# Two-layer decoder trunk on one core: weights laid out by the host unit by unit, one transfer for each unit of 1 MB

## The reference

```python
f = swiglu(rms_norm(h, ffn1_pre_g[i]), ffn1_w_gu[i], ffn1_w_down[i])
h = h + 0.5 * rms_norm(f, ffn1_post_g[i])
u = rms_norm(h, mix_pre_g[i])
sb_q, sb_k, sb_v, df_q, df_k, df_v, g_sb, g_df = jnp.split(u @ w_in[i], split_at, axis=-1)
...
merged = jax.nn.sigmoid(g_sb) * y_sb + jax.nn.sigmoid(g_df) * y_df
h = h + rms_norm(merged @ w_out[i], mix_post_g[i])
f = swiglu(rms_norm(h, ffn2_pre_g[i]), ffn2_w_gu[i], ffn2_w_down[i])
h = h + 0.5 * rms_norm(f, ffn2_post_g[i])
gate = jax.nn.sigmoid(rms_norm(h, ple_pre_g[i]) @ w_ple_gate[i])
h = h + rms_norm((p[i] @ w_ple_proj[i]) * gate, ple_post_g[i])
```

## Time and profile before

| what | before |
|---|---|
| median of 3 runs | 1174.02 us (1173.8 to 1174.78) |
| span of the profiled execution, first to last instruction | 1172.6 us |
| median of the runs less that span | 1.4 us |
| TensorE busy | 1164.0 us (99%) |
| VectorE, ScalarE, GpSimd busy | 850.0, 721.0, 53.0 us |
| DMA | 215.37 MB, mean 184 GB/s, 138655 packets |
| of these, packets under 2 KB | 97904 |

### The profile page before, as it was taken

The page is one execution under the profiler, slowest core; times in us unless marked ns, Lnnn a source line. Parts: engine busy times, 40 slices in busy tenths (PEclk is TensorE's granted clock), DMA queues, the critical chain, the costliest instruction groups (busy, mean ns, idle before and its releaser), DMA issues.

```text
span 1172.6 us, 17196 instructions
## 1 busy us (share of the span) xinstructions
PE 1164.0 (99%) x6031; PEld 983.8 (84%) x6031; DVE 850.0 (72%) x1290; ACT 721.0 (61%) x1166; POOL 53.0 (5%) x124
## 2 busy tenths in 40 slices
PE   9999999999999999999999999999999999999997
PEld 7888888888888888888888888888888888888886
DVE  6766776977857776676787776678776677677666
ACT  7555556577755755555685655565776566565555
POOL 4000000000000000000100000010000010000002
PEclk9999999999999999999999999999999999999999
DMA  9656564654354555655556565746434446546550
GB/s 296 217 181 212 171 215 164 226 172 152 121 201 146 191 204 185 208 174 211 179 171 198 172 211 179 240 165 198 171 111 179 162 162 215 194 170 209 179 196 37
DMA packets 138655, 215.37 MB, mean 184 GB/s; under 512 B 6958, under 2 KB 97904, under 8 KB 138608
## 3 DMA queue, kind: packets, MB, share of 16 engines
q1 hardware_dynamic: 135808, 208.43, 52.6%
q10 hardware_dynamic: 2576, 6.29, 1.6%
q0 software_dynamic: 224, 0.04, 0.0%
HBM read 213.68 MB, written 1.05 MB: 183 GB/s over the span
## 4 chain that ended last, share of the span: by engine, by line
PE 99%; DMA 0%; DVE 0%; ACT 0%; issue 0%; POOL 0%; POOLq 0%; DVEq 0%; ACTq 0%
PE ps L1673 23%; PE ps L1546 19%; PE ps L1548 18%; PE ps L1547 18%; PE ps L1683 12%; PE ps L1916 3%; PE ps L1593 1%; PE ps L1925 1%; PE ps L1802 1%; PE ps L1817 1%; PE ps L1776 0%; PE ps L1788 0%; DMA raw<-in_w_ple_proj 0%; PE ps L1831 0%; PE ps L1838 0%; PE ps L1803 0%
## 5 line engine op out<-in xcount | busy, mean ns | idle before, releaser
L1106 DVE SCALAR_TENSOR_TENSOR w_lo<-raw,g_layer,w_hi 128x512 fp32r<-128x512 f32 (+1 forms) x504 | 356.3, 767 | 139.2 <-ACT w_hi L644 139.2
L644 ACT ACTIVATE w_hi<-raw,g_layer 128x512 fp32r<-128x512 f32 (+1 forms) x524 | 346.7, 732 | 113.6 <-PE ps L1683 97.0
L1673 PE MATMUL ps<-x_both,w_hi 128*128 128x512 f32 x1152 | 287.7, 392 | 0.0
L1673 PEld LDWEIGHTS ps<-x_both,w_hi 128*128 128x128 f32 x1152 | 209.3, 189 | 39.4 <-issue 0.4
L1546 PE MATMUL ps<-w_hi,x_both 128*128 128x512 f32 x576 | 231.6, 402 | 0.0
L1548 PE MATMUL ps<-w_hi,x_both 128*128 128x512 f32 x576 | 225.0, 391 | 0.0
L1547 PE MATMUL ps<-w_lo,x_both 128*128 128x512 f32 x576 | 224.4, 390 | 0.0
L1103 DVE TENSOR_TENSOR w_lo<-raw,w_hi 128x1024 fp32r<-128x1024 f32 x114 | 134.8, 1221 | 61.3 <-ACT w_hi L641 61.3
L641 ACT ACTIVATE w_hi<-raw 128x1024 fp32r<-128x1024 f32 x114 | 114.7, 1053 | 92.7 <-PE ps L1548 92.5
L1683 PEld LDWEIGHTS ps<-x_both,w_lo 128*128 128x128 f32 x1152 | 152.6, 191 | 8.4
L1683 PE MATMUL ps<-x_both,w_lo 128*128 128x256 f32 x1152 | 156.0, 283 | 0.0
(11 more groups left out here) (230 smaller groups left out, 1041.7 us busy)
## 6 DMA issues: line engine op xcount, KB each, us to landing
raw<-in_ffn_w_gu SPq DMA_DIRECT2D x170, 512.0 KB, 4.6
raw<-in_ffn_w_down SPq DMA_DIRECT2D x88, 512.0 KB, 4.0
raw<-in_w_in SPq DMA_DIRECT2D x80, 512.0 KB, 4.5
raw<-in_w_out SPq DMA_DIRECT2D x16, 512.0 KB, 4.1
raw<-in_w_ple_gate SPq DMA_DIRECT2D x16, 512.0 KB, 4.1
raw<-in_w_branch_sb SPq DMA_DIRECT2D x8, 512.0 KB, 4.1
raw<-in_w_branch_diff SPq DMA_DIRECT2D x8, 512.0 KB, 4.2
raw<-in_ffn_w_gu SPq DMA_DIRECT2D x12, 256.0 KB, 7.8
```

The lines of the kernel that those rows point to most:

```text
L644: last = act.activation(w_hi[:, s, part], raw[:, s, part], ACT.Copy, scale=g_layer[:, g:g + 1])
L1106: last = dve.scalar_tensor_tensor(out=w_lo[:, s, part], in0=raw[:, s, part], scalar=g_layer[:, g:g + 1], in1=whi[:, part], op0=ALU.mult, o ...
L1673: mm = pe.matmul(dst, w_hi[:, s, cols], x_both[:, :, 4 * half + k, :], start=half == 0 and k == 0, stop=stop and k == 3, skip_group_check= ...
```

## The change

The ten weight arrays are no longer inputs of the kernel one by one. The host copies them into one array `units` of shape (198, 128, 2048): the 1 MB of a unit lies in one block, and each partition's 2048 values lie in one row of 8 KB, in the order in which the `raw` slot holds them. `load` then issues one DMA of 1 MB for each unit in place of two of 512 KB, and `arrived` counts 16 for each unit in place of 32. The pieces of the first four units stay 256 KB, but each is now 128 rows of 2 KB, for units 1 to 3 too; the rows of a piece lie 8 KB apart in HBM. Slots, waits, the order of the loads, and everything on ScalarE, VectorE and TensorE but the count and the source of two DMAs stay as they are.

```diff
         def arrived(i, u, c=0):
-            return 32 * (UNITS // SLOTS) * i + 32 * c + 32 * (u // SLOTS + 1 - len(range(slot(u), PIECED, SLOTS)))
+            return 16 * (UNITS // SLOTS) * i + 16 * c + 16 * (u // SLOTS + 1 - len(range(slot(u), PIECED, SLOTS)))
...
-        def proj_piece(k):
-            return a["w_ple_proj"][0, (k % 2) * P:(k % 2 + 1) * P, (k // 2) * W:(k // 2 + 1) * W]
+        def unit_of(i, u):
+            return a["units"][i * UNITS + u, :, :]
...
-            def load(i, u, parts, c=0):
+            def load(i, u, c=0):
                 sp_.wait_ge(split_done, UNITS * i + 3 * c + u + 1)
-                for dst, src in parts:
-                    sp_.dma_start(dst, src).then_inc(raw_in[slot(u)], 16)
+                sp_.dma_start(raw[:, slot(u), :], a["units"][bass.ds(3 * c + (i * UNITS + u), 1), :, :].rearrange(
+                    "o p n -> p (o n)")).then_inc(raw_in[slot(u)], 16)
...
             def load_pieces(u, ks=range(4)):
                 for k in ks:
-                    dst = raw[:, slot(u), piece(u, k)]
                     if u == PIECED - 1:
                         sp_.wait_ge(split_done, u + 1)
-                    if u == U_PROJ:
-                        src = proj_piece(k)
-                    else:
-                        c, row = divmod(u - U_FFN1, 2)
-                        dst = dst.rearrange("p (g n) -> p g n", g=2)
-                        src = a["ffn1_w_gu"][0, (4 * row + k) * P:(4 * row + k + 1) * P, :].rearrange(
-                            "p (g n) -> p g n", g=2)[:, :, c * FC:(c + 1) * FC]
-                    sp_.dma_start(dst, src).then_inc(piece_in[u][k], 16)
+                    sp_.dma_start(raw[:, slot(u), piece(u, k)], unit_of(0, u)[:, piece(u, k)]).then_inc(piece_in[u][k], 16)
...
         def _(act):
             for k in (0, 2):
-                act.dma_start(raw[:, slot(U_PROJ), piece(U_PROJ, k)], proj_piece(k)).then_inc(piece_in[U_PROJ][k], 16)
+                act.dma_start(raw[:, slot(U_PROJ), piece(U_PROJ, k)], unit_of(0, U_PROJ)[:, piece(U_PROJ, k)]).then_inc(piece_in[U_PROJ][k], 16)
...
+def laid_units(inputs):
...
+    def deep(name, i, row):
+        units.append(w[name][i, row:row + 2 * P, :].reshape(2, P, D).transpose(1, 0, 2))
+
+    def gate_up(name, i, step, half):
+        rows = w[name][i, half * 4 * P:(half + 1) * 4 * P, :].reshape(4, P, 2, FF)
+        units.append(rows[:, :, :, step * FC:(step + 1) * FC].transpose(1, 0, 2, 3))
...
+    return np.stack([u.reshape(P, UNIT) for u in units])
```

More of the change, by code:

```diff
@@ L455, in load_ffn @@
+            def load_ffn(i, u0):
+                for s in range(3 if (i, u0) != (0, U_FFN1) else 0):
+                    load(i, u0 + s)
+                load(i, u0 + 3)
+                load(i, u0 + 4)
                 with sp_.Fori(2, NC) as c:
[L456 to L459, removed]
+                    for s in range(-1, 2):
+                        load(i, u0 + s, c)
+                load(i, u0 + U_FFN - 1)
@@ L465, in _ @@
                 if i:
[L466 to L481, removed]
+                    load(i, U_PROJ)
+                load_ffn(i, U_FFN1)
+                for u in range(U_WIN, U_FFN2):
+                    load(i, u)
+                load_ffn(i, U_FFN2)
+                for u in range(U_GATE, UNITS):
+                    load(i, u)
             for t in range(TT):
@@ L2093, in _, with ffn @@
                     mm.then_inc(gate_done, 1)
[L2096 to L2100, removed]
+_NAMES = ["x", "p", "positions", "ffn1_pre_g", "ffn1_post_g", "mix_pre_g", "diff_lambda", "diff_subln_g",
+          "mix_post_g", "ffn2_pre_g", "ffn2_post_g", "ple_pre_g", "ple_post_g"]
+def laid_units(inputs):
+    w = {name: np.asarray(inputs[name]) for name in (
+        "ffn1_w_gu", "ffn1_w_down", "ffn2_w_gu", "ffn2_w_down", "w_in", "w_branch_sb", "w_branch_diff", "w_out",
+        "w_ple_gate", "w_ple_proj")}
+    units = []
+    def deep(name, i, row):
[3 more added lines that the diff above has]
+        units.append(rows[:, :, :, step * FC:(step + 1) * FC].transpose(1, 0, 2, 3))
+    def ffn(gu, down, i):
+        for step in range(NC):
+            for half in range(2):
+                gate_up(gu, i, step, half)
+            if step:
+                deep(down, i, (step - 1) * FC)
+        deep(down, i, (NC - 1) * FC)
+    for i in range(DEPTH):
+        deep("w_ple_proj", i, 0)
+        ffn("ffn1_w_gu", "ffn1_w_down", i)
+        for m in range(20):
+            r0, c0 = (m % 2) * 4 * P, W_IN_BLOCK[m // 2] * W
+            units.append(w["w_in"][i, r0:r0 + 4 * P, c0:c0 + W].reshape(4, P, W).transpose(1, 0, 2))
+        for name, n in (("w_branch_sb", 2), ("w_branch_diff", 2), ("w_out", 4)):
+            for s in range(n):
+                deep(name, i, 2 * P * s)
+        ffn("ffn2_w_gu", "ffn2_w_down", i)
+        for s in range(4):
+            deep("w_ple_gate", i, 2 * P * s)
+    return np.stack([u.reshape(P, UNIT) for u in units])
 def kernel(**inputs):
@@ L2107 @@
     nc = bacc.Bacc("TRN2", target_bir_lowering=False, num_devices=1)
+    laid = {name: np.asarray(inputs[name]) for name in _NAMES}
+    laid["units"] = laid_units(inputs)
     arrays, args = {}, {}
-    for name in _NAMES:
-        x = np.ascontiguousarray(inputs[name])
+    for name, x in laid.items():
+        x = np.ascontiguousarray(x)
         arrays[f"in_{name}"] = x
```

## The result

The changed kernel takes 1176.12 us (median of 21 runs, 1175.22 to 1178.23) against 1174.09 us before (21 runs, 1173.59 to 1174.78): a ratio of 1.0019, with a 95% interval of 1.0013 to 1.0025. The forecast was 1173.9 us with a range up to 1175.4 us. The time moved by 2.0 us, within the 0.2% that was called no change, but the median lies 0.7 us above the range: the change costs something, and the forecast had no place for it.

What follows compares the result with a forecast made beforehand. TensorE bounds the kernel, busy 1164.0 of 1172.6 us, never idle in the body. Terms 0 + 0 - 0.1 + 0 on the 1172.6 us span, plus 1.4 us around it, gave 1173.9 us; range 1172.6 to 1175.4 us.

Steps and rivals of the forecast that it cites:

- The count of DMAs: Units 4 to 197 each lose one of two issues, some 92 us of SyncE's queue, beside its waits: 0 on the path.
- the transfer in the body: One 1 MB load lands in 5.4 us, within windows of 12.3 and 6.99 us: cost 0, bounds 0 and 2.2 us.
- The start, first piece: Unit 0's first piece, 3.61 us to landing before the first product at 6.18 us, keeps rows of 2 KB: cost 0.
- The bound of +0.75 us: At the start behind the first piece: one more 256 KB piece let in ahead at 350 GB/s costs at most this.
- The sign that was named: The forecast is wrong if the first product at the start begins over 1 us from 6.18 us.
- The range: Whole kernel: 1172.6 to 1175.4 us, taking in the start's -0.9 and +1.15 us and some scatter; the forecast has 90%.
- The pieces of units 1 to 3: At the start, 390 against 352 GB/s, 0.8 us earlier at the end, not on the path: cost 0, bounds -0.2 and +0.4 us.
- The tile of `x`: At the start, issued at 9.00 us with 1.7 us of room; sharing engines with longer rows could take 0.4 us of it.
- A: Rival on TensorE's matmuls: they get faster as fewer, longer rows disturb memory less; one per cent gives 1162 us; chance 3%.
- B: Rival at the start: the whole chain before the first product gets shorter, giving about 1171 us; chance 2%.
- C: Rival in the body: the single transfer lands too late at the slots' reuse, some 4 us, 1178 us; chance 5%.
- The room there: Narrowest place in the body, 605.13 us, slot read 6.99 us later: 1.6 us of room with a 5.4 us transfer.

Runs made afterwards that it cites:

- The packed: Against the changed kernel, all pieces of units 0 to 3 packed by the host as blocks of 256 KB in the large array: 1174.08 us, ratio 1.0000.
- the padded kernel: Against the changed kernel, every row of the large array padded from 8 to 10 KB, the padding left out of transfers: 1174.16 us, ratio 0.9999.
- the repeat: The changed kernel itself timed again in 11 runs as the yardstick, nothing changed: 1175.83 us, ratio 1.0019 to the kernel before.

## Why the prediction was wrong

- **The count of DMAs and the transfer in the body**, both at 0: right. 194 issues, 4.8 us to landing against 5.4 estimated, windows of 12.3 and 6.99 us, matmuls unchanged. The packed and the padded kernel measure the whole of the rest at ratios of 1.0000 and 0.9999, each within 0.1%.
- **The start, first piece: this is the step that failed.** The prediction said: "It stays 128 rows of 2 KB from the same queue, and only its distance in HBM between rows goes from 4 to 8 KB. Cost 0." The distance was the one thing that counted. The first piece landed in 4.3 in place of 3.6 us (3.8 us in the repeat), piece 2 in 5.8 in place of 4.2 us, and TensorE lost 1.06 us by piece 3. The bound of +0.75 us was drawn from one more piece in the queue, at the full rate of 350 GB/s; but the rate itself fell, to 249 GB/s from 2.5 to 6 us in place of 356 GB/s, and `p` came late with it. The sign that was named, a first product over 1 us late, did not come either: it was 0.66 us late, and the rest was lost before piece 2, to which the prediction gave no line of its own.
- **What the loss sets off** was not in the sum at all: in one profile TensorE's idle time ends with a clock of 0.50 for some 3.5 us, 1.6 us more, and the mean clocks speak for more such runs. The loss of 2.0 us at the median lies between the low runs (1.1 to 1.6 us over before) and the high ones.
- **The range.** It names 0.8 us of scatter above the median, but 1174.0 and 1.15 us leave only 0.25 us for it below the 1175.4 us. With the whole of it the range would have ended at 1175.95 us, still below what was measured.
- **The pieces of units 1 to 3**: the rate of 385 in place of 352 GB/s came, and was worth nothing, as said. But in these units too the distance of 8 KB is slow where they are the first with it, which the kernels with another unit 0 show; the prediction had priced only the gain.
- **The tile of `x`** behind longer rows: it landed in 5.7 us, after 6.5 us before; no crowding.
- **The rivals.** A and B did not come. C named late landings, but in the body and from 7.0 us; its cause, running badly on 8 KB rows, was half right and in the wrong place. The room there was put at 1.6 us and came out at 2.3 us (6.99 less 4.7), while the start had none behind piece 0 and some 0.8 us behind piece 2 (split at 6.82 us, used at 7.66 us): ScalarE already waited 2.2 us for unit 0, and the range should have given that place the price of a slower transfer, not only of a queue.

What was shown: the loss comes from the distance of 8 KB between the rows of the first pieces. What was only argued is why. The Trainium skill, "DMA: Bandwidth & Descriptors", section "Latency and other measured facts", reports the like for copies between tensors in HBM: 207 GB/s with the rows 512 KiB apart, 164 GB/s with 2 MiB and 103 GB/s with 4 and 8 MiB, and 214 GB/s, called full, with 4 KiB of padding added to the 4 MiB, but 97 GB/s with 192 bytes. It infers, without having verified it, that the streams of the partitions run in step and meet in the same parts of memory. The trace agrees in kind, and differs in three points: 8 and 16 KB are slow here (4 KB, a power of two as well, is not), only at the start, and 256 bytes of padding take most of the loss away. That the pieces of units 1 to 3 run at 389 GB/s at the same distance, once unit 0 has come, would fit engines that have fallen out of step by then; no run here shows it. Why 16 KB costs less than 8 KB, and why 4 KB costs nothing, is open too.

## What to carry to other kernels

A layout is more than the length of its rows: when an array is laid out afresh, look at the distance between the rows of the very first transfers, for which there is no cover, and try it padded off the power of two (10 KB in place of 8 KB here), or with each piece packed as one block. Longer rows and fewer transfers are worth nothing where no engine waits for a load, however large the fall in packets. And price a late landing at the start with what it sets off: in one profile TensorE's idle time there cost its clock too, and with that 1.6 us more.

## What the runs showed of the hardware

With rows of 2 KB at a distance of 8 KB the DMA engines moved 249 GB/s from 2.5 to 6 us, in place of 356 GB/s before (rows 4 KB apart), and 389 GB/s from 8 to 9 us in the same run. The slow stretch follows the first pieces with that distance: from 2.8 us in the changed kernel, and at 8 us (124 to 143 GB/s) in three kernels whose unit 0 has another layout. A read of 8 bytes of every row of unit 1 ahead of them did not take it away (1175.27 us). A distance of 10 KB did: 1174.16 us for the whole kernel, against 1174.16 us before on the same chip. While the engines were slow, the tile of `p`, whose rows were as before, landed in 5.1 us in place of 3.8 us. TensorE's idle time of 1.03 us was followed by a granted clock of 0.50 for some 3.5 us; 0.65 us and 1.45 us, at the same place in the program, were not.
